# A one-layer streaming encoder step on one core: x also passed transposed, y returned transposed

## What is computed

```python
n = rms_norm(x, norm1); proj = n @ w_in                 # 1576 columns: u, q, k, v, qi, ki, wi, qm
mix = concat(pool_mixer(u), sparse_attention(q, k, v, ...), memory_attention(qm))
h = x + mix @ w_out                                     # residual
n = rms_norm(h, norm2); up = n @ w_up                   # 2 * 2816 columns
y = h + (silu(gate) * value) @ w_down                   # after a causal convolution of width 3
```

## Time and profile before

| what | value |
|---|---|
| median of 3 runs | 3711.19 us (3708.82 to 3711.97) |
| span of the profiled execution | 3702.1 us |
| PE busy | 3263.2 us, 88% |
| DVE / ACT / POOL busy | 2260.1 / 1078.5 / 785.9 us |
| phase_project, from its first DMA to its last DVE work | about 61 to 565 us |
| phase_mix ch 0 and ch 1, first to last product | 1798 to 1910 us, 2747 to 2863 us |
| end of phase_feed ch 0 and ch 1, behind the last L1663 | 2721 to 2744 us, 3677 to 3699 us |

### The profile page before, as it was taken

One profiled execution on the slowest core, in us unless ns is written; L12 is line 12 of the kernel. 1 busy time (PEld: TensorE's weight loads), 2 busy tenths in 40 slices (PEclk: granted clock), 3 DMA queues, 4 the chain that ended last, 5 costly groups with the idle time before them and its releaser, 6 DMA issues. The chain is left out here.

```text
span 3702.1 us, 51508 instructions
## 1 busy us (share of the span) xinstructions
PE 3263.2 (88%) x19482; PEld 2934.2 (79%) x19482; DVE 2260.1 (61%) x4788; ACT 1078.5 (29%) x1854; POOL 785.9 (21%) x404
## 2 busy tenths in 40 slices
PE   3999985787888887888789999999979899999997
PEld 2777764566666665667689999999969899999997
DVE  5667672777777766684226656656531666666654
ACT  2222222455455544444212221221221211211221
POOL 0000002111000000000245433433214434434420
PEclk7999996999999998999889999999989899999999
DMA  4122225221111010000321111111132211111101
GB/s 138 63 93 84 76 86 151 55 55 33 49 28 28 28 28 25 14 15 13 114 86 35 57 45 34 57 45 34 33 113 75 69 35 45 57 34 45 57 11 48
DMA packets 164909, 202.67 MB, mean 55 GB/s; under 512 B 27775, under 2 KB 138660, under 8 KB 162596
## 3 DMA queue, kind: packets, MB, share of 16 engines
q1 hardware_dynamic: 164772, 200.90, 17.2%
HBM read 155.61 MB, written 45.25 MB: 54 GB/s over the span
## 5 line engine op out<-in xcount | busy, mean ns | idle before, releaser
L1642 DVE SCALAR_TENSOR_TENSOR ffn_gv<-ffn_up,ffn_taps,ffn_gv 128x1056 f32<-128x1056 f32 (+2 forms) x264 | 418.5, 1599 | 157.0 <-ACT ffn_gv L1595 150.6
L1663 DVE TENSOR_TENSOR feed_hT<-feed_hT,ffn_ps_d 128x352 f32<-128x352 f32 x528 | 275.3, 522 | 329.1 <-PE ffn_ps_d L1548 329.1
L1535 PE MATMUL ffn_ps_u<-feed_nhi,feed_up_hi 128*128 128x352 f32 x2112 | 459.7, 326 | 15.8 <-DVE feed_nlo L1673 11.0
L1535 PE MATMUL ffn_ps_u<-feed_nhi,feed_up_lo 128*128 128x352 f32 x2112 | 456.6, 324 | 0.0
L1535 PE MATMUL ffn_ps_u<-feed_nlo,feed_up_hi 128*128 128x352 f32 x2112 | 456.2, 324 | 0.0
L1535 PEld LDWEIGHTS ffn_ps_u<-feed_nhi,feed_up_hi 128*128 128x128 f32 x2112 | 360.9, 190 | 19.3 <-DVE feed_nlo L1673 12.4
L1548 PE MATMUL ffn_ps_d<-ffn_a_hi,ffn_down_hi 128*128 128x352 f32 x1056 | 343.9, 326 | 29.3 <-DVE ffn_a_lo L1654 24.0
L1535 PEld LDWEIGHTS ffn_ps_u<-feed_nhi,feed_up_lo 128*128 128x128 f32 x2112 | 363.8, 188 | 0.0
L1535 PEld LDWEIGHTS ffn_ps_u<-feed_nlo,feed_up_hi 128*128 128x128 f32 x2112 | 360.2, 188 | 0.0
L862 POOL TENSOR_SCALAR att_diag<-ident,keep_w 128x128 f32<-128x128 f32 (+1 forms) x136 | 79.6, 606 | 1310.7 <-PE att_ps_s L892 800.6
L1548 PE MATMUL ffn_ps_d<-ffn_a_lo,ffn_down_hi 128*128 128x352 f32 x1056 | 343.0, 325 | 0.0
(11 more groups left out here) (258 smaller groups left out, 5964.5 us busy)
## 6 DMA issues: line engine op xcount, KB each, us to landing
feed_raw_up<-in_w_up SPq DMA_DIRECT2D x44, 1024.0 KB, 4.9
scratch_sT<-proj_sT SPq DMA_DIRECT2D x16, 1472.0 KB, 5.2
ffn_raw_down<-in_w_down SPq DMA_DIRECT2D x22, 1024.0 KB, 4.9
feed_nlo<-scratch_mixT SPq DMA_DIRECT2D x16, 528.0 KB, 7.7
proj_x<-in_x_prompt SPq DMA_DIRECT2D x16, 512.0 KB, 4.7
att_qi<-scratch_sT SPq DMA_DIRECT2D x16, 512.0 KB, 3.6
att_qa<-scratch_sT SPq DMA_DIRECT2D x16, 512.0 KB, 5.2
att_qb<-scratch_sT SPq DMA_DIRECT2D x32, 256.0 KB, 5.8
```

The lines of the kernel that those rows point to most:

```text
L1535: ins = pe.matmul(ps_u[:, half, s, 0:SUB], a[:, q, k, :], b[:, k, SUB * s:SUB * s + SUB], start=(k == 0 and n == 0), stop=(k == KC - 1 and ...
L1642: ins = dve.scalar_tensor_tensor(gv[:, half, lo:hi], up[:, lo + shift + j - 2:hi + shift + j - 2], taps[:, 2 * j + half, e:e + 1], gv[:, h ...
L1663: dve.tensor_tensor(at, at, ps_d[:, j % 2, 0:SUB], ALU.add).then_inc(partial_read[j % 2], 1)
```

## The change

The host passes `xT`, x transposed (1024 x 2112), beside x, and takes `yT` (1024 x 2112) in place of y. In phase_project xT's columns are loaded (1024 pieces of 512 bytes a block) beside the rows, which are still needed for the sum of squares; both buffers are single now. PE's transposes of x are gone, ACT makes xhi from xT in one copy when the product of the block before is done, POOL makes xlo. ps_x's two PSUM banks go to ps_t, which has four. In phase_mix the residual is one DVE addition of the PSUM tile and a tile of xT, into hT; ACT squares hT. In phase_feed each of the eight tiles of hT is stored to yT when its last addition is done. `row_tiles`, the many small loads, the transposes of y and their copies go. The diff, cut to its core:

```diff
-        x = m.sb("x", [P, 2, D])
+        x = m.sb("x", [P, D])
+        xT = m.sb("xT", [P, KC, P])
...
-        ps_x, ps_g, ps_t = m.ps("ps_x", [P, D]), m.ps("ps_g", [P, 4, 512]), m.ps("ps_t", [P, 2, 512])
+        ps_g, ps_t = m.ps("ps_g", [P, 4, 512]), m.ps("ps_t", [P, 4, 512])
...
-                sp.dma_start(x[0:T, u, :], xrows("x_prompt", "x_sample", "b (n p) d -> (b n) p d", n, T)).then_inc(x_loaded[u], 16)
+                sp.dma_start(x[0:T, :], xrows("x_prompt", "x_sample", "b (n p) d -> (b n) p d", n, T)).then_inc(x_loaded, 16)
...
+            def load_columns(n, u, T):
+                sp.dma_start(xT[:, :, 0:T], t["xT"].rearrange("(c p) r -> p c r", p=P)[:, :, bass.ds(n * P, T)]).then_inc(xT_loaded, 16)
...
-                if not (isinstance(n, int) and n == 0):
-                    sp.wait_ge(xt, n)
-                    sp.wait_ge(squares, n)
-                load_rows(n + 1, 1 - u, TS if isinstance(n, int) and n == NB - 1 else P)
+                sp.wait_ge(x_lo, n + 1)
+                sp.wait_ge(squares, n + 1)
+                rows = TS if isinstance(n, int) and n == NB - 1 else P
+                load_rows(n + 1, 1 - u, rows)
+                load_columns(n + 1, 1 - u, rows)
...
+            def rest(n, u, T, i):
+
+                pool.wait_ge(x_hi, n + 1)
+                pool.tensor_tensor(xlo[:, :, 0:T], xT[:, :, 0:T], xhi[:, :, 0:T].bitcast(F32), ALU.subtract).then_inc(x_lo, 1)
+
+            pipeline(turn=rest, loop=pool.Fori)
...
-                act.wait_ge(xt, n + 1)
-                for h in range(2):
-                    ins = act.activation(xhi[:, 4 * h:4 * h + 4, 0:T], ps_x[:, 512 * h:512 * h + 512].rearrange("p (c n) -> p c n", n=P)[:, :, 0:T], ACT.Copy)
-                ins.then_inc(x_hi, 1)
+                act.wait_ge(xT_loaded, 16 * n + 16)
+                if not (isinstance(n, int) and n == 0):
+                    act.wait_ge(product, 4 * n)
+                act.activation(xhi[:, :, 0:T], xT[:, :, 0:T], ACT.Copy).then_inc(x_hi, 1)
...
-                    src = ps_t[:, 0, :].rearrange("p (s n) -> p s n", n=P)[:, :, 0:T]
+                    src = ps_t[:, g % 4, :].rearrange("p (s n) -> p s n", n=P)[:, :, 0:T]
                     act.activation(sT[:, 4 * g:4 * g + 4, 0:T], src, ACT.Copy).then_inc(read_act, 1)
                 act.wait_ge(turned, N_T * n + 7)
-                act.activation(zT[:, :, 0:T], ps_t[:, 0, 0:256].rearrange("p (s n) -> p s n", n=P)[:, :, 0:T], ACT.Copy).then_inc(read_act, 1)
+                act.activation(zT[:, :, 0:T], ps_t[:, 2, 0:256].rearrange("p (s n) -> p s n", n=P)[:, :, 0:T], ACT.Copy).then_inc(read_act, 1)
...
-            def turn(n, u, T, i):
...
-                    if g >= 2:
-                        pe.wait_ge((read_act, read_dve)[g % 2], 4 * n + g // 2)
+                    if g >= 4:
+                        pe.wait_ge((read_act, read_dve)[g % 2], 4 * n + 1)
                     else:
                         pe.wait_ge((read_act, read_dve)[g % 2], 4 * n)
                     for s in range(min(4, NSLOT - 4 * g)):
-                        ins = pe.transpose(ps_t[:, g % 2, P * s:P * s + T], stack[0:T, 4 * g + s, :].bitcast(F32), ident[0:T, 0:T])
+                        ins = pe.transpose(ps_t[:, g % 4, P * s:P * s + T], stack[0:T, 4 * g + s, :].bitcast(F32), ident[0:T, 0:T])
                     ins.then_inc(turned, 1)
-                pe.wait_ge(read_act, 4 * n + 3)
+                pe.wait_ge(read_act, 4 * n + 2)
...
-                    out = ps_t[HD * (g % 2):HD * (g % 2) + HD, 0, P * (g // 2):P * (g // 2) + T]
+                    out = ps_t[HD * (g % 2):HD * (g % 2) + HD, 2, P * (g // 2):P * (g // 2) + T]
...
-                pe.wait_ge(read_dve, 4 * n + 3)
+                pe.wait_ge(read_dve, 4 * n + 2)
                 for c in range(2):
-                    ins = pe.matmul(ps_t[:, 1, P * c:P * c + T], pool_w[:, c, :], zT[:, c, 0:T], start=True, stop=True)
+                    ins = pe.matmul(ps_t[:, 3, P * c:P * c + T], pool_w[:, c, :], zT[:, c, 0:T], start=True, stop=True)
...
-            def turn(n, u, T, i):
-
-                dve.wait_ge(x_hi, n + 1)
-                for h in range(2):
-                    ins = dve.tensor_tensor(xlo[:, 4 * h:4 * h + 4, 0:T], ps_x[:, 512 * h:512 * h + 512].rearrange("p (c n) -> p c n", n=P)[:, :, 0:T],
-                                            xhi[:, 4 * h:4 * h + 4, 0:T].bitcast(F32), ALU.subtract)
-                ins.then_inc(x_lo, 1)
 
...
-                src = ps_t[:, 1, :].rearrange("p (s n) -> p s n", n=P)[:, :, 0:T]
+                src = ps_t[:, 3, :].rearrange("p (s n) -> p s n", n=P)[:, :, 0:T]
                 for g in (1, 3, 5):
                     k = min(4, NSLOT - 4 * g)
+                    heads = ps_t[:, g % 4, :].rearrange("p (s n) -> p s n", n=P)[:, :, 0:T]
                     dve.wait_ge(turned, N_T * n + g + 1)
-                    dve.tensor_copy(sT[:, 4 * g:4 * g + k, 0:T], src[:, 0:k, :]).then_inc(read_dve, 1)
+                    dve.tensor_copy(sT[:, 4 * g:4 * g + k, 0:T], heads[:, 0:k, :]).then_inc(read_dve, 1)
...
-                        sp.wait_ge(product[u], i)
-                    for r, (_, w, kind, row) in enumerate(tiles):
-                        sp.dma_start(xs[0:w, u, r, :], t[f"x_{kind}"][0, row:row + w, bass.ds((2 * i + u) * P, P)]).then_inc(x_loaded[u], 16)
+                        sp.wait_ge(kept[u], i)
+                    sp.dma_start(xs[:, u, :], t["xT"][bass.ds((2 * i + u) * P, P), HALF * ch:HALF * ch + HALF]).then_inc(x_loaded[u], 16)
...
-                                pe.matmul(ps_h[:, u, s, 0:SUB], a[:, u, k, :], b[:, k, SUB * s:SUB * s + SUB], start=(k == 0 and n == 0), stop=False)
-                    pe.wait_ge(x_loaded[u], 16 * len(tiles) * (i + 1))
-                    for r, (col, w, _, _) in enumerate(tiles):
-                        s, o = col // SUB, col % SUB
-                        ins = pe.matmul(ps_h[:, u, s, o:o + w], xs[0:w, u, r, :], ident[0:w, 0:w], start=False, stop=(o + w == SUB))
+                                ins = pe.matmul(ps_h[:, u, s, 0:SUB], a[:, u, k, :], b[:, k, SUB * s:SUB * s + SUB],
+                                                start=(k == 0 and n == 0), stop=(k == KC - 1 and n == 2))
...
-                    act.wait_ge(product[u], i + 1)
+                    act.wait_ge(kept[u], i + 1)
                     if not first(i):
                         act.wait_ge(added[u], i)
-                    src = ps_h[:, u, :, 0:SUB]
-                    act.activation(sq[:, u, :].rearrange("p (s n) -> p s n", s=NS), src, ACT.Square)
-                    act.activation(hT[:, bass.ds(2 * i + u, 1), :].rearrange("p c (s n) -> p (c s) n", s=NS), src, ACT.Copy).then_inc(kept[u], 1)
+                    act.activation(sq[:, u, :], hT[:, bass.ds(2 * i + u, 1), :].rearrange("p c n -> p (c n)"), ACT.Square).then_inc(squared[u], 1)
...
-            def add(i):
-                for u in range(2):
-                    dve.wait_ge(kept[u], i + 1)
-                    if u:
-                        dve.wait_ge(added[0], i + 1)
-                    elif not first(i):
-                        dve.wait_ge(added[1], i)
-                    dve.tensor_tensor(acc[:, :], acc[:, :], sq[:, u, :], ALU.add).then_inc(added[u], 1)
-
-            iterations(dve, add, KC // 2)
+            def residual(i, u):
+
+                dve.wait_ge(product[u], i + 1)
+                dve.wait_ge(x_loaded[u], 16 * (i + 1))
+                dve.tensor_tensor(hT[:, bass.ds(2 * i + u, 1), :].rearrange("p c (s n) -> p (c s) n", s=NS), ps_h[:, u, :, 0:SUB],
+                                  xs[:, u, :].rearrange("p (s n) -> p s n", s=NS), ALU.add).then_inc(kept[u], 1)
+
+            def total(i, u):
+
+                dve.wait_ge(squared[u], i + 1)
+                if u:
+                    dve.wait_ge(added[0], i + 1)
+                elif not first(i):
+                    dve.wait_ge(added[1], i)
+                dve.tensor_tensor(acc[:, :], acc[:, :], sq[:, u, :], ALU.add).then_inc(added[u], 1)
+
+            def columns(i):
+                residual(i, 0)
+                if not first(i):
+                    total(i - 1, 1)
+                residual(i, 1)
+                total(i, 0)
+
+            iterations(dve, columns, KC // 2, peel=2)
+            total(KC // 2 - 1, 1)
...
-            for i, (_, w, kind, row) in enumerate(out_tiles):
-                sp.wait_ge(y_kept, i + 1)
-                sp.dma_start(t[f"y_{kind}"][0, row:row + w, :], gv[0:w, i % 2, 0:D]).then_inc(stored[i % 2], 16)
-            sp.wait_ge(stored[0], 16 * ((len(out_tiles) + 1) // 2))
-            sp.wait_ge(stored[1], 16 * (len(out_tiles) // 2))
+            for c in range(KC):
+                j = NS * c + NS - 1
+                sp.wait_ge(partial_read[j % 2], 1 + (NIT - 1) * (KC * NS // 2) + j // 2 + 1)
+                sp.dma_start(t["yT"][P * c:P * c + P, HALF * ch:HALF * ch + HALF], hT[:, c, :]).then_inc(stored, 16)
+            sp.wait_ge(stored, 16 * KC)
...
```

(19 more changed lines are left out.)

39 lines of the change are left out of this document (11 added, 28 removed).

## The result

The changed kernel takes 3608.9 us (median of 4 runs, 3601.5 to 3612.1) against 3711.6 for the kernel before: a ratio of 0.9716, 95% interval 0.9702 to 0.9730. A second set of runs, five against nine, gave 0.9711 (0.9698 to 0.9724). The gain is 102.7 us; 118.8 were forecast. The time lies inside the predicted range of 3578 to 3612, near its upper end.

What follows compares the result with a forecast made beforehand. PE, busy 88% of the span, or chains through it set the pace, with DVE's chain nearly level in phase_project. Savings of 52.6 (phase_project), 30.5 (phase_mix) and 35.7 (phase_feed ends) make 118.8; 3711.2 - 118.8 = 3592.4 us, range 3578 to 3612.

Steps and rivals of the forecast that it cites:

- Identity products: phase_mix: removing PE's identity products saves 8 x (2.58 + 2.08) = 37.3 us over both chunks.
- The chain at the end: phase_mix, last product to first sum: 6.7 us with totals blocked beside GpSimd's split, 3.4 more, twice: 6.8 lost.
- Rival A: End of phase_mix: totals are not blocked by POOL's queued split, chain 4.0 us, 5.4 us less, 3587; chance 0.15.
- Ends of phase_feed: Last addition to next stage: 23.0 and 21.3 us shrink to 4.3 each, saving 35.7 us.
- the extra 0.8: Ends of phase_feed: 0.8 us added to the 3.51 us ACT idled, for the new store's larger size, making 4.3.
- the 0.61 of the earlier start: phase_project: without x transposes turn_stack starts at 481.20, once `prepared` is seen, gaining 0.61 us a block.
- The hand-overs: phase_project, turn_stack: four PSUM banks shorten waits on ACT's and DVE's copies, so the band starts 2.80 us sooner.
- DVE's chain: phase_project: a block gains 3.41 us and takes 23.9, bounded by DVE's chain, 0.2 us ahead of the product.
- The moves: phase_project: xlo on POOL and the added xT load cost nothing, except 1 us lost once behind block 0.
- rival C: phase_project: xT's small pieces land late, holding ACT, POOL and product; at 22 us after issue, 3730 us; chance 0.02.
- B: phase_project: turn_stack keeps its length, only 0.61 us a block won, blocks 26.7 us, kernel 3634; chance 0.09.
- The signs of being wrong: PE's product waits elsewhere in steady blocks, the product grows longer, or unchanged stages move over 1 us or two.

Runs made afterwards that it cites:

- the late split: Changed kernel with GpSimd's last split of phase_mix waiting for the last total instead of the last product; 3595.4 us in a single execution.
- the combined kernel: Changed kernel with GpSimd's last phase_mix split late, two filling matmuls ahead of turn_stack's wait for zT, first x rows behind the w_in tiles; 3598.5 us, ratio 0.9679.
- the kernel with the filled wait: Changed kernel with three 128x128 matmuls ahead of the wait for zT in turn_stack; 3603.9 us, ratio 0.9708 to the kernel before.

## Why the prediction was right, and where it was not

**phase_mix, right.** Identity products, forecast 37.3: the stretches of products shortened by 15.8 and 20.3 us, 36.1. The chain at the end, forecast 3.4 longer each: 3.0. Net 30.1 of 30.5. The reason given, totals held beside GpSimd, was tested by taking each side away. By the Trainium skill, SBUF — State Buffer, "Who interferes with whom", a VectorE instruction with two SBUF inputs contends with a GpSimd instruction that reads SBUF, and the one that comes second blocks until the first is done. The traces agree: residual 1.26 us with one SBUF input, totals 2.9 and 3.2 us beside the split and 1.3 alone, each held one ending 1.1 us behind the end of GpSimd's instruction. Rival A is out for this kernel; its 4.0 us is what the late split gives.

**Ends of phase_feed, right.** 37.1 against 35.7; ch 0's end is 4.2 us, ch 1's 3.1, not 4.3. The larger store landed in 2.6 us (page, part 6; 2.7 before), so the extra 0.8 has no slower store behind it; why ch 0 still took 4.2 wasn't looked into.

**phase_project, mechanism right, sum wrong: 40.4 us in its steady stretch where 53.6 stood.** That is below even its own bounds, 45 to 57. Three terms.
- "it starts at 481.20 and gains 0.61", and then "the band starts at 484.17; before, 486.99. That is 2.80 less": the second difference runs from one absolute time to another and already holds the 0.61 of the earlier start. The hand-overs alone are 5.18 - 2.94 = 2.2 us. (486.99 less 484.17 is 2.82; the prediction writes 2.80.) The block gains 2.8 to 2.9, not 3.41. That is 15 x 0.61 = 9.2 us, the largest part of the miss. Blocks without a fall bear it out: 27.3 before, 26.4 with two banks and no x transposes, 24.4 with four. The fifteenth block was counted like the others, but took only 25.3 us before and gained 1.5.
- The clock. The forecast took every duration from blocks at the upper level and supposed that removing work and waits leaves the level alone. Three to four blocks of fifteen fall now, at 0.8 to 1.5 us each: some 4 to 5 us, which the combined kernel got back.
- "With DVE's chain 0.2 ahead of the product as its bound": it was seen rightly as the next bound, and PE waits 0.2 to 0.4 us for it in three and five of the fifteen blocks of the two executions, and in six of the combined kernel's, where no fall delays PE.

**The moves, right.** xlo on POOL took 2.35 us, less than the 3.27 allowed, and nothing waited for it except behind block 0, where the gap grew from 3.7 to 4.2 us. The loss there was put at 1 us; its own terms give 4.82 less 3.15, or 1.7, and it measured 0.5. xT landed in 5.5 us and never held ACT behind block 0; rival C is out, and so is B (26.7).

**The base, right, with a wrong reason.** "The median lies 9.1 us above that span, and I leave this as it is": the base of the forecast is the median, 3711.2, and 3711.6 was measured. But the 9.1 us don't lie outside the profiled program: a span lies 1.8 us under its own time, so the first profile was of a quick execution (its own time isn't on record). Its quickness stood partly in the start of phase_project (65.0 us, against 66.8 to 71.9 in the thirteen other profiles). The gain is 102.7 by the medians, 96.0 by the two first spans and 100.4 by the two later ones.

**The range, kept by its room.** With every stage at its low bound the prediction's own sum gives 3606. The kernel took 3608.9, beyond that, because phase_project missed its bounds and phase_attend was some 5 us longer. It lies under 3612 only by the room that had been added "for what the traces don't show". That is luck in part: the forecast named neither the clock nor phase_attend as what the room was for.

**The signs of being wrong.** Two of the three came. "If the product itself grows longer": it did, in the three or four blocks in which the clock falls. "If the stages between, which the change leaves alone, move by more than 1 us or two": they did, and this was too tight a test. phase_attend, untouched, took 1221.5 to 1224.6 in the three executions with the old phase_project and 1216.5 to 1230.7 in the eleven with the new one. Its time goes with its mean granted clock; two of the extremes, the kernel with the filled wait and the second execution of the changed one:

```profile
528.40:1744.90 1216.50, 986.04 (x5716) 762.29 (x5715) 820.51 (x2303) 567.36 (x1190) 79.61 (x136) 0.94 0.15 40
```

```profile
529.10:1759.70 1230.60, 1000.00 (x5715) 772.42 (x5714) 820.24 (x2303) 567.19 (x1190) 79.44 (x136) 0.92 0.15 39
```

PE is 14 us busier there with the same matmuls, DVE and ACT are not. Whether the new phase_project makes the slower of these more likely (the means are 1222.8 and 1226.4) stays open; three executions on one side are too few.

## What to carry to other kernels

When an early start and a shorter wait are both taken from absolute times of a trace, subtract from one anchor only, or the same time is counted twice. When work or waits are removed from the engine that sets the pace, look for idle gaps that are left beside long stretches of it, and put plain matmuls that fit into the gap there: two of 0.23 us in a gap of 0.47 saved 3 to 5 us over fifteen blocks, a third took most of that back. And where a chain ends a stage, keep GpSimd's work that reads SBUF away from VectorE's instructions with two SBUF inputs: here moving it behind them cost nothing and gave 2.5 us in each of two stages.
